# S5 mixer of a four-layer trunk: turned halves and lag products of the tables as separate steps, masks between the fills

## The reference

```
def s5_mixer(h, a_re, a_im, log_step, b_re, b_im, c_re, c_im, d_skip, w_glu, b_glu):
    lam_bar = exp((a_re + i a_im) * exp(log_step))        # 64 groups x 64 states
    b_bar = (lam_bar - 1) / lam * b                       # 16 channels to 64 states
    bu = einsum('gpc,sbgc->sbgp', b_bar, u)
    x[s] = lam_bar * x[s-1] + bu[s]                       # an associative scan over tokens
    y = real(einsum('gcp,sbgp->sbgc', c, x)) + d_skip * h
    z = gelu(y) @ w_glu + b_glu
    return z1 * sigmoid(z2)
```

## Time and profile before

| what | us |
|---|---|
| median of 3 runs | 1676.58 (1671.02 to 1678.82) |
| span of the profiled execution | 1676.4 |
| TensorE busy | 1497.3 (89%) |
| VectorE busy | 1031.8 (62%) |
| ScalarE busy | 750.2 (45%) |
| GpSimd busy | 619.4 (37%) |
| S5 tables, first fill to last y product | about 911 to 1044.5 |

### The profile page before, as it was taken

One profiled execution on the slowest core, in us unless ns is written; L12 is line 12 of the kernel. 1 busy time (PEld: TensorE's weight loads), 2 busy tenths in 40 slices (PEclk: granted clock), 3 DMA queues, 4 the chain that ended last, 5 costly groups with the idle time before them and its releaser, 6 DMA issues.

```text
span 1676.4 us, 32397 instructions
## 1 busy us (share of the span) xinstructions
PE 1497.3 (89%) x13606; PEld 1389.3 (83%) x13606; DVE 1031.8 (62%) x1565; ACT 750.2 (45%) x1185; POOL 619.4 (37%) x300
## 2 busy tenths in 40 slices
PE   5989899997998885899997568989999898989998
PEld 5888899985887773899986457979999787989998
DVE  4595477736284458477788766356762389357752
ACT  3466465532412332465541111455553357555643
POOL 5222366740010010386741000336764232237663
PEclk9999899998899997999998668999999999999999
DMA  5433355562342001375552001435556343335553
GB/s 150 151 126 102 101 177 187 183 183 75 106 145 77 4 10 44 102 209 187 177 163 70 1 1 39 135 105 184 192 169 198 110 142 101 127 123 180 176 190 112
DMA packets 212801, 210.07 MB, mean 125 GB/s; under 512 B 12272, under 2 KB 211904, under 8 KB 212672
## 3 DMA queue, kind: packets, MB, share of 16 engines
q1 hardware_dynamic: 210784, 206.65, 38.2%
q0 software_dynamic: 832, 1.13, 0.4%
q10 hardware_dynamic: 1056, 0.43, 0.1%
HBM read 207.15 MB, written 1.05 MB: 124 GB/s over the span
## 4 chain that ended last, share of the span: by engine, by line
PE 74%; DVE 17%; ACT 4%; issue 3%; ACTq 1%; POOL 1%; DMA 0%; DVEq 0%; POOLq 0%
PE psum L370 15%; PE psum L371 15%; PE psum L372 15%; PE psum L644 6%; PE psum L454 5%; DVE work L2145 4%; PE psum L646 3%; DVE w_low L353 3%; ACT w_high L345 2%; PE psum L2076 1%; PE psum L390 1%; PE psum L1345 1%; DVE work L1103 1%; PE psum L1456 1%; PE psum L1442 1%
## 5 line engine op out<-in xcount | busy, mean ns | idle before, releaser
L353 POOL TENSOR_TENSOR w_low<-ring,w_high 128x1024 fp32r<-128x1024 f32 (+1 forms) x184 | 511.4, 2780 | 921.0 <-ACT w_high L345 886.0
L370 PE MATMUL psum<-x_high,w_high 128*128 128x256 f32 x2048 | 593.2, 290 | 45.7 <-issue 31.0
L371 PE MATMUL psum<-x_low,w_high 128*128 128x256 f32 x2048 | 588.0, 287 | 0.0
L372 PE MATMUL psum<-x_high,w_low 128*128 128x256 f32 x2048 | 587.7, 287 | 0.0
L345 ACT ACTIVATE w_high<-ring 128x1024 fp32r<-128x1024 f32 (+1 forms) x368 | 361.8, 1034 | 262.1 <-PE psum L372 165.9
L370 PEld LDWEIGHTS psum<-x_high,w_high 128*128 128x128 f32 x2048 | 401.7, 196 | 53.1 <-issue 36.3
L371 PEld LDWEIGHTS psum<-x_low,w_high 128*128 128x128 f32 x2048 | 402.0, 196 | 1.0 <-issue 1.0
L372 PEld LDWEIGHTS psum<-x_high,w_low 128*128 128x128 f32 x2048 | 401.9, 196 | 0.0
L353 DVE TENSOR_TENSOR w_low<-ring,w_high 128x1024 fp32r<-128x1024 f32 (+1 forms) x184 | 251.8, 1370 | 176.9 <-ACT w_high L345 176.5
L730 DVE SCALAR_TENSOR_TENSOR work<-psum,par,work 128x255 f32<-128x255 f32 (+1 forms) x352 | 145.4, 475 | 155.1 <-ACT work L669 154.9
L644 PE MATMUL psum<-inner,w_high 128*128 128x512 f32 x528 | 186.5, 398 | 2.7 <-DVE w_low L353 2.7
(11 more groups left out here) (299 smaller groups left out, 1860.6 us busy)
## 6 DMA issues: line engine op xcount, KB each, us to landing
ring<-in_ffn_w_up_dram SPq DMA_DIRECT2D x88, 1024.0 KB, 5.1
ring<-in_ffn_w_down_dram SPq DMA_DIRECT2D x32, 1024.0 KB, 5.2
ring<-in_dsa_w_in_dram SPq DMA_DIRECT2D x28, 1024.0 KB, 5.2
ring<-in_ffn_w_down_dram SPq DMA_DIRECT2D x16, 768.0 KB, 4.6
ring<-in_rwkv_w_rkv_dram SPq DMA_DIRECT2D x12, 1024.0 KB, 5.1
ring<-in_dsa_w_out_dram SPq DMA_DIRECT2D x8, 1024.0 KB, 5.1
ring<-in_s_w_glu_dram SPq DMA_DIRECT2D x8, 1024.0 KB, 5.4
ring<-in_rwkv_w_out_dram SPq DMA_DIRECT2D x4, 1024.0 KB, 5.2
```

The source lines that it names most:

```text
L353: eng.tensor_tensor(low, raw, high.bitcast(F32), ALU.subtract).then_inc(sem("w_split", b), 1)
L370: pe.matmul(out_, lhs[0], rhs[0], start=start, stop=False, skip_group_check=True)
L371: pe.matmul(out_, lhs[0], rhs[1], start=False, stop=False, skip_group_check=True)
L372: return pe.matmul(out_, lhs[1], rhs[0], start=False, stop=stop, skip_group_check=True)
```

## The change

`tables(i)` is split. `turned_table(i)` does the transposes and signals ft_turned, `lag_table(i)` does the lag products and signals lag_full. TensorE's order for each q becomes: four turned tables, states(q), the first lag table, from_states(q-1), the other three lag tables, from_inputs(q). On VectorE, `toeplitz` now masks one table, and `fill` takes a function that is called in its middle and at its end: the masks of quarter q-1 stand there, while quarter q is filled. scan(q-1) follows the fills of quarter q. Mask 12 stands inside scan(2), mask 13 behind it, mask 14 inside scan(3) and mask 15 behind it.

The rest of the diff merges semaphores. a_full and c_full become params_turned, step_exp with mag_done and sin_done become powers_ready, sigma_done and angle_done become angles_ready, par_cleared and chunk_constants join constants, xt_full and out_full become x_turned; abs_done, gelu_done, rstd and z_ready become marks on an engine's own step semaphore; the increments of warm and r1_done are dropped.

```
-            def tables(i):
+            def turned_table(i):
                 q, g0 = i // 4, i % 4 * 2
                 if i % 4 == 0:
...
                 for e in range(2):
                     for v in range(2):
                         at = (2 * e + v) * P
-                        pe.transpose(banks[4][:, at:at + P], FB[:, q, v, g0 + e], ident[:, :])
+                        mm = pe.transpose(banks[4][:, at:at + P], FB[:, q, v, g0 + e], ident[:, :])
+                mm.then_inc(sem("ft_turned"), 1)
+
+            def lag_table(i):
+
+                q, g0 = i // 4, i % 4 * 2
                 if i % 4 == 0:
                     pe.wait_ge(sem("gc_done"), q + 1)
                 if i:
                     pe.wait_ge(sem("toeplitz"), i)
...
-                mm.then_inc(sem("ft_full"), 1)
+                mm.then_inc(sem("lag_full"), 1)
...
             for q in range(4):
                 for i in range(4 * q, 4 * q + 4):
-                    tables(i)
+                    turned_table(i)
                 states(q)
-                from_inputs(q)
+                lag_table(4 * q)
                 if q:
                     from_states(q - 1)
+                for i in range(4 * q + 1, 4 * q + 4):
+                    lag_table(i)
+                from_inputs(q)
             from_states(3)
...
-            def fill(dst, raw, q, c_re, c_im, signal_):
+            def fill(dst, raw, q, c_re, c_im, signal_, between):
...
                 step.mark(dve.tensor_tensor(out_[0], out_[0], t, ALU.subtract))
+                between(0)
                 tt(out_[1], re, y, ALU.mult)
...
                 dve.wait_ge(sem(signal_), q + 1)
-
-            def toeplitz(q):
-
-                for i in range(4 * q, 4 * q + 4):
-                    g0 = i % 4 * 2
-                    dve.wait_ge(sem("ft_full"), i + 1)
...
+                between(1)
+
+            def toeplitz(i):
+
+                q, g0 = i // 4, i % 4 * 2
+                dve.wait_ge(sem("lag_full"), i + 1)
...
-            def scan(q):
+            def scan(q, between=lambda: None):
...
-                ins.then_inc(sem("z_ready"), 1)
-                dve.wait_ge(step.sem, step.n)
-                dve.wait_ge(sem("z_ready"), q + 1)
+                    else:
+                        dve.wait_ge(step.sem, step.mark(ins))
+                between()
                 turn(Z, q)
...
             for q in range(4):
-                fill(FB, b_raw, q, FB_RE, FB_IM, "fb_done")
-                fill(GC, c_raw, q, GC_RE, GC_IM, "gc_done")
+                masks = (lambda k, q=q: toeplitz(4 * (q - 1) + k)) if q else (lambda k: None)
+                fill(FB, b_raw, q, FB_RE, FB_IM, "fb_done", masks)
+                fill(GC, c_raw, q, GC_RE, GC_IM, "gc_done", lambda k: masks(2 + k))
                 if q:
-                    toeplitz(q - 1)
-                if q > 1:
-                    scan(q - 2)
-            scan(2)
-            toeplitz(3)
-            scan(3)
+                    scan(q - 1, (lambda: toeplitz(12)) if q == 3 else (lambda: None))
+            toeplitz(13)
+            scan(3, lambda: toeplitz(14))
+            toeplitz(15)
...
             for i in range(16):
-                act.wait_ge(sem("ft_full"), i + 1)
+                act.wait_ge(sem("ft_turned"), i + 1)
```

More of the change, by code:

```diff
@@ L378, in norm_squares @@
                 if m == 3:
-                    act.activation(warm[:, n:n + 1], eps[:, 0:1], ACT.Sqrt).then_inc(sem("warm"), 1)
+                    act.activation(warm[:, n:n + 1], eps[:, 0:1], ACT.Sqrt)
                 act.wait_ge(sem("x_ready"), 4 * n + m + 1)
@@ L713, in pair @@
                 if before_s5(L) and j == UP_TILES // 2 - 1:
-                    dve.wait_ge(sem("a_full"), 1)
+                    dve.wait_ge(sem("params_turned"), 1)
                     dve.tensor_copy(small(A_RE, 2), banks[6][:, 0:2 * S5_H]).then_inc(sem("a_ready"), 1)
@@ L1813, in rp @@
                     rr = rT[:, hp, :].rearrange("p (t i c) -> p t i c", t=TT, i=2)
-                    dve.tensor_tensor(rr, rr, each[:, :, :, 0, :], ALU.add).then_inc(sem("r1_done"), 1)
+                    dve.tensor_tensor(rr, rr, each[:, :, :, 0, :], ALU.add)
                     dve.tensor_tensor(PT_all[:, hp, 0].rearrange("p (t i) j -> p t i j", t=TT), each[:, :, :, 1, :],
@@ L1956, in s5_exponentials @@
                 for v in range(2):
-                    act.wait_ge(sem("c_full"), v + 1)
+                    act.wait_ge(sem("params_turned"), 1 + v + 1)
                     act.activation(c_raw[:, v].rearrange("p g c -> p (g c)"), banks[7 - v][:, :],
@@ L1960, in s5_exponentials @@
                 act.wait_ge(sem("s5_in", 0), 16 * S5_DMAS[0])
-                act.activation(small(STEP), small(STEP), ACT.Exp).then_inc(sem("step_exp"), 1)
+                act.activation(small(STEP), small(STEP), ACT.Exp).then_inc(sem("powers_ready"), 1)
             if part == 1:
-                act.wait_ge(sem("sigma_done"), 1)
+                act.wait_ge(sem("angles_ready"), 1)
                 for k in range(S5_L):
                     for first, s in ((MAG_N, -1.0), (MAG_P, 1.0)):
[L1967 to L1971, removed]
+                        act.activation(small(first + k), small(SIGMA), ACT.Exp, scale=s * (k + 1)).then_inc(sem("powers_ready"), 1)
+                act.wait_ge(sem("angles_ready"), 2)
+                size = scalar_step.mark(act.activation(small(CO_ARG), small(ANGLE), ACT.Abs))
+                act.activation(small(U_IM), small(ANGLE), ACT.Sin).then_inc(sem("powers_ready"), 1)
+                act.wait_ge(scalar_step.sem, size)
                 act.activation(small(U_RE), small(CO_ARG), ACT.Sin, bias=half_pi[:, 0:1],
-                               scale=-1.0).then_inc(sem("sin_done"), 1)
+                               scale=-1.0).then_inc(sem("powers_ready"), 1)
         def s5_act(act, L):
@@ L2022, in s5_turn_a @@
                 mm = pe.transpose(banks[6][:, v * S5_H:(v + 1) * S5_H], a_rows[:, v], ident[0:S5_H, 0:S5_H])
-            mm.then_inc(sem("a_full"), 1)
+            mm.then_inc(sem("params_turned"), 1)
         def s5_turn_c(pe):
@@ L2031, in s5_turn_c @@
                     mm = pe.transpose(banks[7 - v][:, b * P:(b + 1) * P], c_rows[:, v, b], ident[:, :])
-                mm.then_inc(sem("c_full"), 1)
+                mm.then_inc(sem("params_turned"), 1)
         def s5_pe(pe, L):
@@ L2072, in tables @@
                 for e in range(2):
+                    at = e * P
                     for v in range(2):
@@ L2178, in s5_tables @@
             if part == 0:
-                dve.wait_ge(sem("step_exp"), 1)
+                dve.wait_ge(sem("powers_ready"), 1)
                 dve.wait_ge(sem("a_ready"), 1)
                 tt(small(TH), small(A_IM), small(STEP), ALU.mult)
-                dve.tensor_tensor(small(SIGMA), small(A_RE), small(STEP), ALU.mult).then_inc(sem("sigma_done"), 1)
+                dve.tensor_tensor(small(SIGMA), small(A_RE), small(STEP), ALU.mult).then_inc(sem("angles_ready"), 1)
                 big_ = 1.5 * 2.0 ** 23
@@ L2192, in s5_tables @@
                 dve.tensor_scalar(small(ANGLE), small(ANGLE), 3.1415925, -3.1415925, ALU.min,
-                                  ALU.max).then_inc(sem("angle_done"), 1)
+                                  ALU.max).then_inc(sem("angles_ready"), 1)
             if part == 1:
@@ L2198, in s5_tables @@
                 then(dve.reciprocal(small(DEN), small(DEN)))
-                dve.wait_ge(sem("sin_done"), 2)
+                dve.wait_ge(sem("powers_ready"), 1 + 16 + 2)
             for p, have in ((2, 1), (2, 2), (3, 4)):
@@ L2205, in s5_tables @@
             if part == 4:
-                dve.wait_ge(sem("mag_done"), 16)
+                dve.wait_ge(sem("powers_ready"), 1 + 16)
                 tt(small(B_RE), small(MAG_P), small(U_RE), ALU.mult)
@@ L2409, in then @@
                 pool.wait_ge(step.sem, step.mark(ins))
-            pool.memset(par_rows[:, PAR_BLOCKS - 1, :], 0.0).then_inc(sem("par_cleared"), 1)
+            pool.memset(par_rows[:, PAR_BLOCKS - 1, :], 0.0).then_inc(sem("constants"), 1)
             pool.memset(ident[:, :], 0.0).then_inc(step.sem, 1)
@@ L2458, in chunk_constants @@
             then(pool.memset(half_pi[:, :], TWO_PI / 4))
-            pool.tensor_copy(head_eye[HALF:P, :], ident[HALF:P, HALF:P]).then_inc(sem("chunk_constants"), 1)
+            pool.tensor_copy(head_eye[HALF:P, :], ident[HALF:P, HALF:P]).then_inc(sem("constants"), 1)
         def load_pe(pe):
-            pe.wait_ge(sem("constants"), 1)
+            pe.wait_ge(sem("constants"), 2)
             pe.wait_ge(sem("x_in"), 32)
@@ L2468, in load_pe @@
                 if c % 2:
-                    mm.then_inc(sem("xt_full"), 1)
+                    mm.then_inc(sem("x_turned"), 1)
             pe.wait_ge(sem("par_in"), 16 * par_dmas(FAST_PAR))
@@ L2480, in load_dve @@
             for m in range(4):
-                dve.wait_ge(sem("xt_full"), m + 1)
+                dve.wait_ge(sem("x_turned"), m + 1)
```

(12 more changed lines are left out.)

16 lines of the change are left out of this document (7 added, 9 removed).

## The result

The changed kernel takes 1698.15 us (median of 4 runs, 1691.68 to 1700.96), the kernel before 1677.7 us beside it. The ratio is 1.0116, 95% interval 1.0095 to 1.0138: slower, as forecast, by little over 1%. The forecast was 1690.8 us, +14.2; measured is about +19.5 by the ratio, inside the range of 1675 to 1703 but in its upper part. The profiled execution has a span of 1694.9 us, 18.5 over before.

A forecast was written before the change was run, and what follows sets the result against it. The prediction took the chain on TensorE and VectorE, which wait for each other, as the bound. Quarters ending at 938.1, 951.7, 982.9 and 1015.4 and a tail to 1058.7 (before 1044.5) gave +14.2 on 1676.4: 1690.8 us, range 1675 to 1703.

The forecast's parts named there:

- Signals cost nothing: Merged semaphores keep each wait at the same point and dropped increments had no reader; cost zero.
- A: S5 stage, a quarter's last mask to the next quarter's first lag product: 17.1 us, 12.3 at full clock, 20.0 at half.
- A is not covered, and the waits move to the first masks: VectorE fills only 9.35 us of 17.1; first-mask waits of 8.8, 7.8, 9.1 and 13.6 us, 39 in all.
- The 25 us of waits between masks go: VectorE's 8.44 us of mask waits in each of three quarters go, hidden by fills: 25.3 us of possible gain.
- The tail is one chain: Last quarter: scans alternate with products instead of lying beside them; last y product at 1058.7, before 1044.5.
- At most 0.5 us at the other masks: VectorE, masks after a quarter's first: second mask waits 0.5 us, 4.85 of TensorE work against 4.3 of mask and half fill.
- Terms inside A: TensorE: from_inputs 6.2, four turned tables 6.3, states 3.2, lag product 1.4, together 17.1 us.
- The term that was too small: TensorE's from_states: 3.68 us at full clock in middle quarters, 4.5 for from_states(2) in the tail.
- The rule on transposes: Turned tables all at half clock, 7.2 us, and states 3.63: 1.3 more in four quarters, 1696; left out of the sum.
- Rival "the clock stays full": Pauses of 0.7 us in the turned tables do not drop TensorE's clock; 1669 to 1685 us, tail 34.7, chance 0.20.
- the fall at 961.40: Profile before: TensorE, with one table between pauses (0.66 us of work in 2.59), kept full clock only to 961.40.

The follow-up runs named there:

- e1: Kernel before with only the changed kernel's merged signals, order of the S5 stage as before; ratio to before 0.9997, stage 117.5 us.
- e6: Changed kernel with the tables of quarter q+1 turned between the lag tables of quarter q on TensorE, VectorE as changed; ratio to before 0.9934, stage 102.2 us.
- e7: Changed kernel with the masks of quarter q-1 together behind the fills of quarter q, last quarter as changed; ratio to before 1.0047, stage 124.4 us.
- e5: Changed kernel with its last quarter in the old order on VectorE and TensorE, scan(2) whole before masks 12 to 15; ratio to before 1.0073, tail 39.5 us.
- e10: Changed kernel with extra unused matmuls in TensorE's pauses, 2 behind each table's transposes and 2 or 10 behind lag tables; ratio to before 0.9978, stage 111.3 us.

## Why the prediction was right, point by point

The direction and the mechanism held, and the size came out 5 us short. The range held it with 5 to 7 us to spare.

- *Signals cost nothing*: right as far as can be measured (e1).
- *A is not covered, and the waits move to the first masks*: right in mechanism and size. A was 16.8 us (17.1 said), and in quarter 2, with ScalarE's weight rounding on its path, 17.9 (18.4 said); the four first-mask waits are within 0.5 us of those said. e6 and e7 take the wait away from two sides, by shortening A and by covering it, and the time falls each time.
- *The 25 us of waits between masks go*: right, but e7 shows that it is the wrong gain to look for: grouped masks behind a covered A wait only 1.3 to 2.2 us each.
- *The tail is one chain*: right, 44.1 us (43.3 said). e5 took 4.6 of it off, where I expected 10.
- *At most 0.5 us at the other masks*: wrong. Masks 5, 9 and 13 waited 1.55, 2.07 and 7.53, 11.2 us together, which is why all waits are 50.4 and not 39. Part of that is a slip in the list and not in the sum: the prediction's own tail puts from_states(2) and a lag product, 5.9 us, ahead of mask 13.
- *Terms inside A*: the sum was near because errors cancelled, and that was luck. Turned tables took 5.4 and not 6.3 in quarters 1 and 3, all at full clock (in quarter 2 the last table, behind the late copy, took 0.88). The lag table behind states took 2.08 and not 1.4, states 3.2 to 3.6 where I had 3.2. A as a whole came out 0.3 to 0.5 under the sum.
- *The term that was too small*: from_states. I priced from_states(q-1) at 3.68, full clock; it took 4.79 and 5.32. from_states(2) took 6.34 where I had taken 4.5. With lag table 4q+1 behind it, masks 5 and 9 waited 1.55 and 2.07 (0.5 said) and mask 13 waited 7.53. In the middle quarters it stands behind a lag table that ran at half clock (2.08), and the prediction gave no reason for the full-clock price; in the tail it stands behind a pause of 2.98. The three were 1.1, 1.6 and 1.8 us too small, 4.6 together. The three A gave 1.1 back, quarter 0 added 0.6 (its lag table took 2.08, not 1.4), and the rest, mostly in the tail, gave 0.8 back; so the stage came out 3.3 longer than summed (135.7 against 132.4).
- *The rule on transposes*: the Trainium skill ("TensorE: Matmul & The Clock Gate", Part 4: PE-mode transpose) says that the full clock does not engage for transposes, which do not count as activity the way matmuls do. By it the prediction put the turned tables at half clock. Behind a from_inputs that had reached the full clock they ran at 1.00 for 5.37 us, with the clock falling right behind, so the trace of quarters 1 to 3 does not bear out that price; whether transposes alone would raise the clock no run shows. The sum by that rule, 1696, should have been about 1695, since quarter 0 was already priced at half, and that it lies nearer to the measured time is luck: the tables did not cost what it charges. In e10 two matmuls in each pause held the clock through states (2.06). Whether it falls by the transposes or by the pauses isn't told apart by that, since the calls both fill pauses and are matmuls.
- *Rival "the clock stays full"*: did not happen by itself, but e10 made it happen, and its sum was right: 34.85 us of tail against 34.7. TensorE's longest pause in the changed stage was 2.98 us, most were 0.7 to 2.3, and the clock was still 0.67. Against it spoke the fall at 961.40, and rightly.

## What to carry to other kernels

Before putting work between two waits to cover them, add up what the *first* of the waits needs on the other engine, and put the cover ahead of that; cover behind the longest wait hides little. When two engines hand work back and forth, let the producer run a quarter ahead at the point where its input is first full. And on a stage full of short pauses price TensorE's work at half clock, or check how much a kernel gains by filling the pauses with useless matmuls: that tells how much of a loss is clock and how much is order.

## What the runs showed of the hardware

The same 32 matmuls of from_inputs took 3.68 us or, behind work broken by pauses of 0.8 to 3 us, 5.1 to 6.5. Adding 264 matmul instructions to the stage (1224 against 960) raised its clock from 0.67 to 0.98 and made the kernel about 23 us faster, 24 of the stage's 136. A run of four tables' transposes with equally long pauses (0.66 us each, 0.69 between) kept the full clock for 5.4 us behind from_inputs, and it fell within the following matmuls. It also surprised me that a pause of 0.70 us per table, taken away, was worth 11 us and not the 7 to 9 of its own sum; the clock of the stage rose with it from 0.71 to 0.82.
